# Gate sums, decayed queries and keys, masked scores and the split of the output weight in the chunk stage of a one-core hybrid SSD, GLA and mixture-of-experts layer

## The reference, cut to what matters

```python
def ssd_scan(x, dt, Bm, Cm, A, h0, with_output):      # 8 heads of 64, chunks of 128 tokens
    a_cs = jnp.cumsum(dtc * A, axis=2)
    w_end = jnp.exp(a_end[:, :, None] - a_cs) * dtc
    chunk_states = jnp.einsum('bcjh,bcjhn,bcjhp->bchpn', w_end, Bc, xc)
    # h = decay * h + s, over the chunks
    scores = jnp.einsum('bcihn,bcjhn->bcijh', Cc, Bc) * decay_ij * dtc
    y = einsum(scores, xc) + einsum(Cc, h_in) * jnp.exp(a_cs)[..., None]
...
def gla_scan(q, k, v, g, S0, with_output):            # 4 heads, keys 64, values 128, chunks of 64 tokens
    b = jnp.cumsum(g, axis=2)
    chunk_states = jnp.einsum('bcjhk,bcjhv->bchkv', kc * jnp.exp(b_end - b), vc)
    q_dec = qc * jnp.exp(b)
    k_inv = kc * jnp.exp(-b)
    attn = jnp.where(causal, jnp.einsum('bcihk,bcjhk->bchij', q_dec, k_inv), 0.0)
    o = einsum(attn, vc) + einsum(q_dec, S_in)
...
def merge_heads(m, y_ssd, o_gla, p):
    y = rmsnorm((y_ssd + p['d_skip'] * x) * silu(z), p['ssd_norm_g'])
    o = rmsnorm(o_gla, p['gla_norm_g']) * silu(g_out)
    return jnp.concatenate([y, o], axis=-1) @ p['w_out']
...
x = x + m_lat[2] * mix_lat                            # gated residual, then a second norm, the router and the experts
```

## Time and profile before

| | us |
|---|---|
| median of 3 runs | 2832.84 |
| lowest and highest | 2830.89, 2845.7 |
| the profiled execution, its own time | 2829.67 |
| its span in the trace | 2827.9 |
| stage `chunks` in the span | about 929 to 1087 |
| stage `mixer`: set-up and step 0 | about 1090.5 to 1171.8 |
| stage `mixer`: steps 1 to 15 | 1171.8 to 1689.1 |
| stage `mixer`: the last two steps | 1689.1 to 1724.3 |

### The profile page before, as it was taken

How to read it: one execution, slowest core, us unless ns; L and a number is a source line. 1 busy time by engine, 2 the same in 40 slices (tenths; PEclk the granted TensorE clock), 3 DMA queues, 4 the chain that set the end, 5 groups by cost and what they waited for, 6 DMA issues and landing times. The chain is left out here.

```text
span 2827.9 us, 36830 instructions
## 1 busy us (share of the span) xinstructions
PE 2456.4 (87%) x12303; PEld 1857.3 (66%) x12303; DVE 1546.5 (55%) x1960; ACT 1064.9 (38%) x1315; POOL 529.4 (19%) x535
## 2 busy tenths in 40 slices
PE   2999999999999796689998883299999999999990
PEld 1677567656665564577777772278888888888880
DVE  1322122222212344555555555199999999999993
ACT  0112112121212121322222220177777777777772
POOL 1000000000000001112212212523333333333332
PEclk7899999989999676689999996599999999999995
DMA  8122212111210567444444436144789876989976
GB/s 315 56 69 80 92 41 84 73 61 65 98 43 12 215 216 263 178 161 161 168 161 161 162 109 217 41 151 135 227 286 311 271 251 208 364 264 355 316 258 260
DMA packets 174733, 492.19 MB, mean 174 GB/s; under 512 B 11504, under 2 KB 26251, under 8 KB 167467
## 3 DMA queue, kind: packets, MB, share of 16 engines
q1 hardware_dynamic: 150971, 407.67, 39.3%
q0 software_dynamic: 23664, 83.18, 11.9%
HBM read 382.16 MB, written 108.65 MB: 174 GB/s over the span
## 5 line engine op out<-in xcount | busy, mean ns | idle before, releaser
L578 PE MATMUL pz<-w_in_sb,hT 128*128 128x512 f32 x800 | 367.9, 621 | 0.0
L548 PE MATMUL pf<-hT,w_in_sb 128*128 128x256 f32 x1440 | 331.1, 395 | 1.1 <-DVE hT L637 1.1
L548 PEld LDWEIGHTS pf<-hT,w_in_sb 128*128 128x128 f32 x1440 | 286.7, 200 | 42.8 <-DVE hT L637 1.5
L1912 ACT ACTIVATE w_hi_e<-w_gates 128x2048 fp32r (+1 forms) x103 | 197.6, 1919 | 236.4 <-issue 103.1
L578 PEld LDWEIGHTS pz<-w_in_sb,hT 128*128 128x128 f32 x800 | 158.1, 200 | 191.9 <-issue 191.5
L2038 DVE TENSOR_TENSOR w_lo_e<-w_gates,w_hi_e 128x2048 fp32r<-128x2048 f32 x103 | 236.7, 2299 | 33.3 <-ACT w_hi_e L1912 33.3
L2038 DVE TENSOR_TENSOR w_lo_e<-w_ups,w_hi_e 128x2048 fp32r<-128x2048 f32 x102 | 233.4, 2288 | 35.6 <-ACT w_hi_e L1912 35.6
L2038 DVE TENSOR_TENSOR w_lo_e<-w_downs,w_hi_e 128x2048 fp32r<-128x2048 f32 x100 | 228.2, 2282 | 0.0
L1912 ACT ACTIVATE w_hi_e<-w_ups 128x2048 fp32r (+1 forms) x102 | 195.2, 1914 | 23.8 <-PE pd_e L1985 22.6
L1912 ACT ACTIVATE w_hi_e<-w_downs 128x2048 fp32r x100 | 191.1, 1911 | 3.0 <-issue 0.3
L1985 PE MATMUL pg_e<-w_hi_e,x_hi_e 128*128 128x512 f32 x408 | 167.3, 410 | 7.2 <-DVE w_lo_e L2038 7.2
(11 more groups left out here) (348 smaller groups left out, 4285.9 us busy)
## 6 DMA issues: line engine op xcount, KB each, us to landing
w_gates<-in_w_gate_dram SPq DMA_DIRECT2D x32, 2048.0 KB, 11.5
w_ups<-in_w_up_dram SPq DMA_DIRECT2D x32, 2048.0 KB, 16.6
w_downs<-in_w_down_dram SPq DMA_DIRECT2D x32, 2048.0 KB, 10.3
tok_rec<-tm SPq DMA_DIRECT2D x8, 2960.0 KB, 9.6
rec_m<-tok_rec SPq DMA_DIRECT2D x16, 1288.0 KB, 7.2
rec_s<-tok_rec SPq DMA_DIRECT2D x18, 968.0 KB, 6.7
w_mod_half<-in_w_mod_dram SPq DMA_DIRECT2D x16, 1024.0 KB, 7.9
abc_m<-a_rows SPq DMA_DIRECT2D x16, 1024.0 KB, 9.9
```

The source lines that it names most:

```text
L548: mm = pe.matmul(pf[n % 2][:, f, :], w[:, k, c0:c0 + P], h[:, k, :], start=(k == 0), stop=(k == KT - 1))
L578: mm = pe.matmul(pz[n % 2][:, :], h[:, k, s * P:(s + 1) * P], w[:, k, o:o + 512], start=(k == 0), stop=(k == KT - 1))
L1912: act.activation(w_hi[:, s % 3:s % 3 + 1, :], raw(part, half, place), ACT.Copy).then_inc(hi_done, 1)
```

## The change

Work moves from `mixer` to `chunks`, in five parts, and the mixer's lists are put in a new order.

- The gate sums are formed in `chunks` for all columns (`sums_t`, the product of the gate record with `incl_bd`) in place of the chunk ends alone (`halves`); the four 64-column `ones` products become one of 128 columns. `small` loses its second buffer, so that `sums(i)` waits for ScalarE's reads of tile i-1.
- `chunks` loads `feat` too, exponentiates the gate sums (`grow`, and the inverse), multiplies queries and keys (`decayed_qk`), forms and masks the C.B scores (`masked_scores`), and stores the three as `qk_rec`, 768 KB a tile.
- `chunks` splits the output weight: `gated_w` and `low_w` on VectorE, the high part on ScalarE, a slice a step from step 3 to 11; `w_hi` and `w_lo` outlive the stage.
- The mixer loads `qk_rec` and one row block of `feat_rec` (`cT`) instead of `feat` and the gate columns of `rec`; `z` and `g_out` come in a load of their own (`zg`). Tile n+1's load is issued in step n. The fills of `h_rows` are issued one a step.
- The decay matrices of tile n+1 (`front`: `segment`, `decayed_scores`, `decayed_c`) are formed in step n. `attn` and `gla`, and the state products of `chunks`, run their loops in another order of heads and halves.

```diff
@@ chunks @@
-        small = [ps(f"small{b}") for b in range(2)]
+        small, sums_t = ps("small"), ps("sums_t")
 ...
+            def load(i):
+                sp.dma_start(rec[i % NR][:, :], tok_rec[at(i)][:, 0:T_Z]).then_inc(loaded[i % NR], 16)
+                sp.dma_start(feat[i % NR][:, :, :]..., feat_rec[at(i)]).then_inc(loaded[i % NR], 16)
 ...
+                if i >= CT:
+                    sp.wait_ge(qk_done, 2 * (i - CT) + 2)
+                    sp.wait_ge(scm_done, 2 * (i - CT) + 2)
+                    sp.dma_start(qk_rec[at(i)], qk[i % 2]...).then_inc(qk_stored[i % 2], 16)
+                if NW <= i < KT:
+                    sp.wait_ge(w_lo_done, i - NW + 1)
+                    load_w(i)
 ...                                                    (ScalarE)
+                act.activation(grow[i % 3][:, :, :], g, ACT.Exp).then_inc(grow_done, 1)
+                if i >= CT:
+                    act.activation(qk[b][:, 1, :, :], g, ACT.Exp, scale=-1.0).then_inc(grow_done, 1)
 ...
+                if W0 <= j < W0 + KT:
+                    act.activation(w_hi[:, k, :], w_raw[k % NW][:, :], ACT.Copy).then_inc(w_hi_done, 1)
 ...                                                    (TensorE, sums)
+                if i >= 1:
+                    pe.wait_ge(ends_done, 3 * i)
+                    pe.wait_ge(grow_done, i + max(0, i - CT))
 ...
-                        mm = pe.matmul(small[b][:, 20 + 8 * d + 2 * pair:22 + 8 * d + 2 * pair], r[:, ...], C["halves"][:, :], ...)
+                        mm = pe.matmul(sums_t[:, P * (2 * d + pair):P * (2 * d + pair + 1)], r[:, ...], incl_bd[:, :], ...)
 ...
+                pe.matmul(small[:, 16:32], C["ones"][:, :], dta[b][:, :], start=True, stop=True).then_inc(sums_ps, 1)
 ...                                                    (TensorE, products)
+                if i - 1 >= CT:
+                    pe.wait_ge(scm_done, 2 * (i - 1 - CT) + 2)
+                    if i >= CT:
+                        pe.matmul(sc, f[64 * g:64 * g + 64, 0, :], f[64 * g:64 * g + 64, 1, :], start=True, stop=True)
-                    for c, to in ((0, second), (1, first)) if d else ((0, first), (1, second)):
-                        for h in range(GH):
+                    for h in range(GH):
+                        for c, to in ((0, second), (1, first)) if d else ((0, first), (1, second)):
 ...                                                    (VectorE)
             for j in range(TILES + 1):
                 if j < TILES:
                     log_decays(j)
                 if j >= 1:
                     weighted(j - 1)
+                    decayed_qk(j - 1)
                 if j >= 2:
                     states(j - 2)
+                    masked_scores(j - 2)
+                if W0 < j <= W0 + KT:
+                    low_w(j - W0 - 1)
+                if W0 <= j < W0 + KT:
+                    gated_w(j - W0)
@@ mixer @@
-            for n, part in enumerate((2, 4, 3)):
+            for n, part in enumerate((4, 3)):
 ...                                                    (SyncE)
             for n in range(LT + 1):
                 if now is not None and now + 1 < LT:
                     sp.wait_ge(lag_done, 4 * now + 4)
                     load_abc(now + 1)
+                    if before is not None:
+                        sp.wait_ge(o_ps, before + 1)
+                        sp.wait_ge(next_done, before + CT + 1)
+                    load(now + 1)
+                    if before is not None:
+                        sp.wait_ge(o_done, before + 1)
+                    load_zg(now + 1)
                     sp.wait_ge(y_ps, now + 1)
                     load_cs(now + 1)
 ...                                                    (GpSimd)
-            for t in range(LT):
-                pool.dma_start(h_t[t], shift_bc[:, :]).then_inc(rows_filled, 16)
+                    pool.dma_start(h_t[now], shift_bc[:, :]).then_inc(rows_filled, 16)
 ...                                                    (ScalarE, one step)
+                if before is not None:
+                    squares_o(before)
+                    split_m(before, 0)
+                    split_m(before, 1)
                 if done is not None:
                     turned_x(done)
                 if now is not None:
                     squares_y(now)
                     normed_y(now)
+                    if now + 1 < LT:
+                        decays(now + 1, 0)
+                        decays(now + 1, 1)
+                        inter_decays(now + 1)
                 if before is not None:
                     squares_x(before)
 ...                                                    (TensorE, one step)
-                    scores(now)
-                    turned_m(before)
+                if before is not None:
+                    turned_m(before, 0)
+                if now is not None:
+                    attn(now)
+                    ssd(now)
+                if before is not None:
+                    turned_m(before, 1)
                 if done is not None:
                     turned_x(done)
                 if before is not None:
                     project(before, range(0, 4))
                 if done is not None:
                     router(done)
-                if now is not None:
-                    ssd(now)
-                    attn(now)
                 if before is not None:
                     project(before, range(4, KT))
                 if now is not None:
                     gla(now)
 ...                                                    (VectorE, one step)
+                if now is not None:
+                    masked_attn(now)
+                if before is not None:
+                    split_m(before, 0)
+                    gated_o(before)
+                if now is not None:
+                    state_mid(now + CT, now)
+                    state_next(now + CT, now)
+                if before is not None:
+                    split_m(before, 1)
+                if now is not None:
+                    gated_y(now)
+                if done is not None:
+                    logits(done)
+                if now is not None and now + 1 < LT:
+                    front(now + 1)
+                if before is not None:
+                    residual(before)
+                    scaled_x(before)
```

More of the change, by code:

```diff
@@ L146, in build @@
             return
-        chunks(nc, A, C, tok_rec, back_state, fwd_chunk, a_rows)
+        held = ExitStack()
+        w_hi, w_lo = (held.enter_context(nc.sbuf_tensor(n, [P, KT, D], mybir.dt.float32r)) for n in ("w_out_hi", "w_out_lo"))
+        chunks(nc, A, C, w_hi, w_lo, tok_rec, feat_rec, back_state, fwd_chunk, qk_rec, a_rows)
         if "stop2" in debug:
             return
-        mixer(nc, A, C, route, tok_rec, feat_rec, back_state, fwd_chunk, a_rows, x_mid, h_rows)
+        mixer(nc, A, C, w_hi, w_lo, route, tok_rec, feat_rec, back_state, fwd_chunk, qk_rec, a_rows, x_mid, h_rows)
+        held.close()
         if "stop3" in debug:
@@ L857, in products @@
             def products(i):
-                r, k, x = rec[i % NR], kend[i % 2], xw[i % 2]
+                r, k, x, f = rec[i % NR], kend[i % 2], xw[i % 2], feat[i % NR]
                 pe.wait_ge(kend_done, i + 1)
                 pe.wait_ge(xw_done, i + 1)
-                for d, ssd, first, second, done in ((1, b02[:, 0:256], b02[:, 256:512], b1[:, 0:256], back_ps),
-                                                    (0, f01[:, 0:256], f01[:, 256:512], f2[:, 0:256], fwd_ps)):
+                if i - 1 >= CT:
+                    pe.wait_ge(scm_done, 2 * (i - 1 - CT) + 2)
@@ L863, in products @@
+                for d, ssd, first, second, sc, done in ((1, b02[:, 0:256], b02[:, 256:512], b1[:, 0:256], b1[:, 256:256 + P], back_ps),
+                                                        (0, f01[:, 0:256], f01[:, 256:512], f2[:, 0:256], f2[:, 256:256 + P], fwd_ps)):
                     if i:
-                        pe.wait_ge(*((next_done, i) if d else (fwd_done, 2 * i)))
+                        pe.wait_ge(*((next_done, i) if d else (fwd_done, 4 * i)))
+                    if i >= CT:
+                        g = 1 - d
+                        pe.matmul(sc, f[64 * g:64 * g + 64, 0, :], f[64 * g:64 * g + 64, 1, :], start=True, stop=True)
@@ L911, in weighted, with decayed_qk, masked_scores @@
                                   ALU.mult).then_inc(xw_done, 1)
+            def decayed_qk(i):
+                if i < CT:
+                    return
+                f, b = feat[i % NR], i % 2
+                dve.wait_ge(grow_done, i + 1 + i + 1 - CT)
+                if i >= CT + 2:
+                    dve.wait_ge(qk_stored[b], stores(i, b, 2))
+                for n, e in ((0, grow[i % 3][:, :, :]), (1, qk[b][:, 1, :, :])):
+                    src = f[:, 2 + 2 * n:4 + 2 * n, :].rearrange("p a b -> p (a b)").unsqueeze(1).to_broadcast([P, 2, 2 * P])
```

(24 more changed lines are left out.)

358 lines of the change are left out of this document (157 added, 201 removed).

## The result

The changed kernel takes 2854.81 us (median of 17 runs, 2844.72 to 2864.0) against 2836.76 us for the kernel before (17 runs): ratio 1.0064, 95% interval 1.0044 to 1.0084. It is slower by about 0.6%, where 2724 us was forecast. Its profiled execution took 2862.16 us, with a span of 2860.2 us.

The account below looks back on a forecast made before the run. The prediction took TensorE to be full nearly everywhere, except for holes. Mixer steps -97.5, set-up and step 0 -33 and `chunks` +22 summed to -108.5 us, from 2832.84 to 2724 us, range 2680 to 2778.

Parts of the forecast that it names:

- the mixer's set-up: Mixer set-up and step 0: the 22.1 us before `gla(0)` go whole; sum -33 us, bounds -28 and -38.
- The part on new waits: `chunks`: `sums(i)` waits about 0 in steady state, 2.7 us at the start; `products(i)` waits for `masked_scores(i-1)`.
- a bound of +55: `chunks`: upper bound of its +22 us growth, with all 16 steps at 11.9 us instead of 8.5.
- The weight split: `chunks`: in eight steps VectorE binds full-clock steps at 8.3 to 8.6 us instead of 6.5, not slow ones.
- The clock in `chunks`: `chunks`: added waiting brings more slow steps, half of the eight with weight that are fast today.
- `chunks` at 1.2 GHz throughout: Rival, chance 0.12: `chunks` grows by 55 us instead of 22, total 2757 us.
- TensorE's list in the mixer: Mixer steps 1 to 15: TensorE's new list sums to 26.2 us at full clock.
- The load loop, "I add 0.4": Mixer steps: load, `front`, `residual` and `scaled_x` take 24.6 to 26 us, about TensorE's list; 0.4 us added.
- the decay matrices are not really ahead: Rival, chance 0.10: late loads let `front` delay the mixer's `residual`; steps 30.5 us, total 2761 us.
- The clock surcharge: Mixer steps: 1.4 us a step kept for clock drops, as in the steps before.
- the two rivals together: `chunks` at 1.2 GHz and decay matrices not ahead, chance 0.03: about 2795 us.
- All three signs: Wrong if mixer steps exceed 30 us, `residual` starts late because `front` ran late, or `chunks` grows beyond 55 us.

Follow-up runs that it names:

- c1: Changed kernel with three buffers instead of two for the record of decayed queries, keys and masked scores in `chunks`: 2794.1 us.
- c2: Changed kernel, still two buffers, with the `qk_rec` store issued ahead of the next tile's loads in `chunks`: 2796.3 us.
- b1: Changed kernel with the edits of c1, m1 and m2 together: 2731.0 us.
- b2: b1 with the residual also put ahead of the decayed scores on VectorE: 2706.9 us.
- b5: b2 with the `chunks` store of queries, keys and scores also issued ahead of the next tile's loads: 2704.9 us.
- m1: Changed kernel whose mixer `segment` and attention parts on VectorE wait only for the three transfers they read, on their own semaphore: 2833.3 us.
- m2: Changed kernel with the mixer's load of x moved behind the next step's loads in SyncE's queue: 2798.7 us.
- m3: Changed kernel with the mixer's residual put ahead of the decayed scores in VectorE's order: 2815.7 us.
- b6: Changed kernel with only the two SyncE queue moves of c2 and m2: 2737.5 us.
- m4: Changed kernel with GpSimd's weighted x in the mixer made to wait until VectorE's segment passes are done: 2867.3 us.

## Why the prediction was wrong

- **What bounded the kernel, and the mixer's set-up:** right. Set-up and step 0 lost 33.7 us, 33 forecast, and the wait of 22.1 us before `gla(0)` is gone.
- **`chunks`, the step that failed most.** The part on new waits named `sums(i)` for ScalarE's reads and `products(i)` for the masked scores, and stopped there. The change adds a third: L855 and L999 wait for the landing of `qk_rec`'s store. I listed that store's bytes and divided them by a bandwidth; I did not follow it as a DMA that somebody waits for, with two buffers, and with the loads ahead of it in SyncE's list. Forecast +22 with a bound of +55, measured +92; c1 and c2 each give about 60 us of the total back. In their profiled executions the stage grew by 24 and 46 us, so the rest of this term was near. The bytes fitted in the stage, yet the loop through one transfer didn't.
- **The weight split:** the mechanism was right and the size close. VectorE does bind the full-clock steps that hold it, at 7.93 us instead of 8.3 to 8.6, and not the slow ones. It hardly ever bound the changed kernel, though: one step took 7.93 us (decayed end keys at 958.35 and 966.28), and from then on the store held all but the last two.
- **The clock in `chunks`:** the direction was right (more slow steps). With the wait gone a slow step is 12.6 us, against the 11.9 that my upper bound took. The rival "`chunks` at 1.2 GHz throughout" came true from 1040 us on, but as a companion of the wait: from 1000 to 1050 us c1, without it, was granted 0.70 and the changed kernel 0.50. c2 and b1 had long stretches at 0.50 without the wait, though, so how much of the slow clock the wait brought isn't shown.
- **TensorE's list in the mixer:** right. 26.2 us forecast at full clock, 25.8 measured in b2; `gla` 3.3 instead of 3.9, `attn` 1.09 instead of 0.9. The means of b2 and b5, 26.2 and 26.3 us, are so near the forecast because their clock cost 0.4 us a step and not 1.4.
- **The load loop, "I add 0.4":** this term was mis-sized. A step was forecast at 28.0 us and took 32.6, 4.6 more, 69 us in all (28.9 gained instead of 97.5); 4.0 of the 4.6 are this loop. I had written the loop down as 24.6 to 26 us. It took 30.6: 3.7 from the transposes to the end of `scaled_x`, 16.2 for the transfers (11.1 forecast), 9.9 for `front` (7.6 forecast), 0.8 for the first half of the residual. (`front` is ten passes of about 0.6 us and one of 1.2, 7.4 us; the twelve of the prediction would make 8.4, not its 7.6. The three beside GpSimd's passes added 2.5.) The transfers were sized at 433 GB/s, the best 4 us of the earlier trace rows. Over the whole landing they made:

```profile
1526.20:1542.30 16.10, 14.69 (x109) 12.82 (x109) 6.91 (x15) 3.03 (x6) 3.58 (x6) 1.00 0.97 322
1532.00:1542.30 10.30, 9.51 (x49) 8.09 (x50) 2.12 (x5) 2.10 (x5) 0.79 (x2) 1.00 1.03 362
```

- That is 322 GB/s (5.2 MB) at a DMA share of 0.97, and 362 in the fullest 10 us. The figure of about 358 GB/s for HBM to SBUF, from the Trainium skill ("DMA: Bandwidth & Descriptors", "Where 436 GB/s comes from"), which the prediction set aside, is the nearer one over 10 us; the trace's 433 is a peak of 4 us. By that figure the loop was said to be 27 to 28.5 us, still short of 30.6: the whole landing took 2.8 us more than the 13.4 worked out with it, and `front` 2.3 more than forecast.
- **The rival "the decay matrices are not really ahead" (0.10)** is what the mixer did: `front` delays `residual`, 32.6 us a step instead of its 30.5. It was to decide once records land over 14 us into a step; they landed 19.9 us into it. m1, m2 and m3 each cut the loop in another place and each gave 1.5 to 3.8 us a step. The clock surcharge, kept at 1.4, also grew, to 2.0 over the loop of 30.6: 0.84 granted over the steps, 0.94 once m2 let TensorE run through.
- **The range** took the two rivals together at 2795. With the measured terms for `chunks` (+92 instead of +22) and the steps (-29 instead of -97.5) and its own -33 for the set-up, the prediction's sum is 2829.67 + 92 - 33 - 29 = 2859.7; the profiled execution took 2862.16. The last two steps, put at 0, cost 2.8. All three signs that the prediction named for its being wrong came: steps over 30 us, a `residual` that starts late because `front` ran late, `chunks` grown by more than 55.
- The forecast of 2724 us is near what the change brings with its transfers well placed: b6, with two moved and nothing else, took 2737.5, b1 2731.0, b2 2706.9.

## What to carry to other kernels

When a change adds a store, ask who next writes into its buffer: count the buffers, and follow the chain from the last writer through everything ahead of the store in its queue, to its landing and back. When work is moved an iteration ahead, its loads move too: their issue, the landing at the bandwidth of a whole window (not of its best microseconds), the work behind it and what stands behind that work on the same engine must fit into one step. Most of both losses here was undone by moving one transfer each within one queue (b6, 117 us).

## What the runs showed of the hardware

- TensorE ran at the 0.50 clock for 67 us while it was busy for all of them (c2). So it isn't only waiting that keeps it there; when it rises again stays open, since the same code had 169.4 us in one execution (c1) and 184.0 in another (b1).
- A pass on VectorE with two inputs from SBUF takes 0.68 us alone and 1.4 to 1.6 beside GpSimd's passes, and m4 moved this from one group of passes to the other. The Trainium skill ("SBUF — State Buffer", "Who interferes with whom") has the two share a port pair that one instruction holds until its end. The trace nearly agrees: in the changed kernel's step above VectorE's first pass, started 0.01 us after GpSimd's of 1.04 us, took 1.58; one after the other they would take 1.04 + 0.68 = 1.72. GpSimd's next two, beside VectorE's, took 1.49 each.
- The landing of one and the same store of 768 KB was 9.9 us behind 1.35 MB of loads and 4.4 us ahead of them.
